# GpSimd makes the low part of a weight piece in two halves of 512 columns, and TensorE waits for each half

## The reference, cut to what matters

```python
for l in range(2):                                   # first block
    x = x + 0.5 * rmsnorm(swiglu(rmsnorm(x, g), w_gate[l], w_up[l], w_down[l]), g)   # 1024 -> 2816 -> 1024
    x = x + rmsnorm(token_mixing(rmsnorm(x, g), w_in[l], ..., w_out[l]), g)          # three kinds of attention
    x = x + 0.5 * rmsnorm(swiglu(...), g)
for l in range(2):                                   # second block
    x = x + merged(rms_norm(x), mem, ...) @ w_out[l]      # sparse, gated-linear and memory attention
    x = x + square(relu(rms_norm(x) @ w_up[l])) @ w_down[l]                          # 1024 -> 4096 -> 1024
```

## Time and profile before

| | |
|---|---|
| median of 3 runs | 1881.97 us (1881.95 to 1882.25) |
| the profiled execution | 1882.18 us, span 1880.7 us |
| TensorE busy | 1874.1 us (100%), weight loads 1549.2 us (82%) |
| GpSimd busy | 1554.2 us (83%) |
| ScalarE, VectorE busy | 1035.2 us, 1032.0 us (55% each) |
| weights read | 346.11 MB, 185 GB/s |

### The profile page before, as it was taken

One profiled execution on the slowest core, in us unless ns is written; L12 is line 12 of the kernel. 1 busy time (PEld: TensorE's weight loads), 2 busy tenths in 40 slices (PEclk: granted clock), 3 DMA queues, 4 the chain that ended last, 5 costly groups with the idle time before them and its releaser, 6 DMA issues.

```text
span 1880.7 us, 27121 instructions
## 1 busy us (share of the span) xinstructions
PE 1874.1 (100%) x9604; PEld 1549.2 (82%) x9604; DVE 1032.0 (55%) x2654; ACT 1035.2 (55%) x1765; POOL 1554.2 (83%) x1091
## 2 busy tenths in 40 slices
PE   9999999999999999999999999999999999999999
PEld 8888887888888889788888877888888877788887
DVE  5438465533676756554444677446444477645542
ACT  7445666444644476654466454665456554566543
POOL 8988876988798878698879787779887968778986
DMA  7665534666675554367556343456757443355664
GB/s 290 238 231 185 163 134 158 194 196 191 206 236 192 192 167 136 133 218 260 194 189 252 124 146 119 151 184 218 237 191 264 164 127 132 125 167 190 192 195 140
DMA packets 98419, 348.94 MB, mean 186 GB/s; under 512 B 13260, under 2 KB 13932, under 8 KB 97772
## 3 DMA queue, kind: packets, MB, share of 16 engines
q1 hardware_dynamic: 97708, 346.06, 55.2%
q10 hardware_dynamic: 576, 1.14, 0.2%
HBM read 346.11 MB, written 1.05 MB: 185 GB/s over the span
## 4 chain that ended last, share of the span: by engine, by line
PE 98%; POOL 1%; DVE 0%; ACT 0%; issue 0%; ACTq 0%
PE psum L642 28%; PE psum L644 28%; PE psum L643 28%; PE psum L670 1%; PE psum L672 1%; PE psum L673 1%; PE psum L911 1%; PE psum L728 1%; PE psum L901 1%; PE psum L924 1%; PE psum L1170 1%; POOL lo L615 1%; PE psum L891 0%; PE psum L1327 0%; PE psum L1121 0%; PE psum L798 0%
## 5 line engine op out<-in xcount | busy, mean ns | idle before, releaser
L615 POOL TENSOR_TENSOR lo<-raw,hi 128x256 fp32r<-128x256 f32 (+1 forms) x1081 | 1546.4, 1454 | 308.5 <-ACT hi L1475 280.8
L1475 ACT ACTIVATE hi<-raw 128x1024 fp32r<-128x1024 f32 (+1 forms) x613 | 639.3, 1053 | 498.2 <-PE psum L644 460.9
L642 PE MATMUL psum<-hi,h_hi 128*128 128x512 f32 (+1 forms) x1504 | 593.0, 394 | 0.5 <-POOL lo L615 0.5
L644 PE MATMUL psum<-hi,h_lo 128*128 128x512 f32 (+1 forms) x1504 | 583.6, 388 | 0.0
L643 PE MATMUL psum<-lo,h_hi 128*128 128x512 f32 (+1 forms) x1504 | 583.0, 388 | 0.0
L2177 DVE STREAM_TRANSPOSE psum<-big 32x128 f32<-32x128 f32 (+1 forms) x960 | 344.0, 358 | 14.2
L642 PEld LDWEIGHTS psum<-hi,h_hi 128*128 128x128 f32 x1504 | 282.5, 188 | 61.7 <-POOL lo L615 2.7
L644 PEld LDWEIGHTS psum<-hi,h_lo 128*128 128x128 f32 x1504 | 282.3, 188 | 58.6
L642 PE MATMUL psum<-hi,y_hi 128*128 128x512 f32 x832 | 328.1, 394 | 0.0
L643 PEld LDWEIGHTS psum<-lo,h_hi 128*128 128x128 f32 x1504 | 282.7, 188 | 55.0
L644 PE MATMUL psum<-hi,y_lo 128*128 128x512 f32 x832 | 324.3, 390 | 0.0
(11 more groups left out here) (354 smaller groups left out, 1568.7 us busy)
## 6 DMA issues: line engine op xcount, KB each, us to landing
raw<-in_stream SPq DMA_DIRECT2D x607, 512.0 KB, 4.2
big<-in_w SPq DMA_DIRECT2D x14, 512.0 KB, 7.3
big<-in_post SPq DMA_DIRECT2D x6, 512.0 KB, 5.1
special<-in_b_merge SPq DMA_DIRECT2D x2, 1536.0 KB, 8.2
raw<-in_stream SPq DMA_DIRECT2D x8, 296.0 KB, 6.4
memkv<-in_mem_turned SPq DMA_DIRECT2D x2, 1024.0 KB, 6.3
big<-in_band SPq DMA_DIRECT2D x2, 768.0 KB, 6.3
raw<-in_first SPq DMA_DIRECT2D x2, 512.0 KB, 4.3
```

Source lines behind the costliest of these rows:

```text
L615: t = pool.tensor_tensor(M.lo[:, slot, w], M.raw[:, slot, w], f32(M.hi[:, slot_hi, w]), ALU.subtract)
L642: pe.matmul(out, lhs_hi, rhs_hi, start=start, stop=False)
L644: return pe.matmul(out, lhs_lo, rhs_hi, start=False, stop=stop)
L1475: act.activation(M.hi[:, slot_hi, used], M.raw[:, slot, used], ACT.Copy).then_inc(sem["hi"], 1)
```

## The change

Pieces from 3 on that are outside the mixers' strips and of full width (449 of them) are now two instructions of 512 columns on GpSimd. The left one raises "half_lo", the right one "lo". TensorE waits for "half_lo" ahead of the left columns and for "lo" ahead of the right ones. Quartered and narrow pieces, the end of a gated feed-forward and `high_first` wait as before. In `enter`, the wait for a piece is left out for the second token tile.

```diff
+def by_halves(c):
+    return c >= FIRST_HALVES and not in_mixer(c) and half_width(c) == PIECE // 2
+
+def halves_until(c):
+    return FIRST_HALVES + sum(by_halves(i) for i in range(FIRST_HALVES, c + 1))
...
         pool.wait_ge(sem["hi"], c + 1)
+        if by_halves(c):
+            for i in range(2):
+                w = slice(512 * i, 512 * i + 512)
+                pool.tensor_tensor(M.lo[:, slot, w], M.raw[:, slot, w], f32(M.hi[:, slot_hi, w]),
+                                   ALU.subtract).then_inc(sem["lo"] if i else sem["half_lo"], 1)
+            continue
...
+    def wait_left(c):
+        if by_halves(c):
+            pe.wait_ge(sem["half_lo"], halves_until(c))
+        else:
+            pe.wait_ge(sem["lo"], c + 1)
+
+    def wait_right(c):
+        if by_halves(c):
+            pe.wait_ge(sem["lo"], c + 1)
...
     def strip_piece(c, j, a_hi, a_lo, bank, memory=None):
-        pe.wait_ge(sem["lo"], c + 1)
+        wait_left(c)
...
         for i in range(2):
+            if i:
+                wait_right(c)
...
     def rows(...):
-        pe.wait_ge(sem["lo"], c + 1)
+        wait_left(c)       # and wait_right(c) between the halves of m == 0
...
     def half_rows(c, m, kt, a_hi, a_lo, banks, stop):
         if m == 0:
-            pe.wait_ge(sem["lo"], c + 1)
-        t = rows_tile(c, m, kt, a_hi, a_lo, banks, False, stop)
+            wait_left(c)
+        t = rows_tile(c, m, kt, a_hi, a_lo, banks, False, stop, lambda: None if m else wait_right(c))
...
     def enter(...):
-                pe.wait_ge(sem["lo"], c + j + 1)
+                if m == 0:
+                    wait_left(c + j)       # and wait_right between the halves, in strip_tile and rows_tile
```

More of the change, by code:

```diff
@@ L687, in rows, with right_half @@
     def rows(c, kt, a_hi, a_lo, banks, start, stop=False, second=lambda: None, right=lambda m: None):
-        pe.wait_ge(sem["lo"], c + 1)
+        def right_half(m):
+            if m == 0:
+                wait_right(c)
+            right(m)
+        wait_left(c)
         for m in range(MT):
@@ L692, in rows @@
                 second()
-            t = rows_tile(c, m, kt, a_hi, a_lo, banks, start, stop, lambda: right(m))
+            t = rows_tile(c, m, kt, a_hi, a_lo, banks, start, stop, lambda: right_half(m))
             if stop and m == 0:
@@ L735, in enter @@
             for j in range(4):
-                pe.wait_ge(sem["lo"], c + j + 1)
+                if m == 0:
+                    wait_left(c + j)
                 pe.wait_ge(sem["xlo"], 8 * f + 4 * m + pair_of(j) + 1)
@@ L748, in strip_tile @@
         for i in range(2):
+            if i and m == 0:
+                wait_right(c)
             k, w = 2 * j + i, slice(i * 512, i * 512 + 512)
@@ L1415, in mix2 @@
                 enter(V.merged, (0, 1, 2, 3), "merged", 4 * layer, c,
-                      lambda cc, m, j: rows_tile(cc, m, j, h_hi, h_lo, (4, 6), j == 0, False), lambda j: j // 2)
+                      lambda cc, m, j: rows_tile(cc, m, j, h_hi, h_lo, (4, 6), j == 0, False,
+                                                 lambda: None if m else wait_right(cc)), lambda j: j // 2)
                 pe.wait_ge(sem["xlo"], 8 * n["feats"])
```

## The result

The changed kernel is slower. Five runs of it have a median of 1890.76 us (1889.64 to 1890.95), the kernel before took 1882.14 us beside them (1881.95 to 1882.91). The ratio on record is 1.0042, 95% interval 1.0031 to 1.0053; the two medians themselves stand 8.6 us or 0.46% apart. The forecast was 1880.1 us and "no change"; the result lies outside its range and on the side that had a chance of 0.05. The profiled execution took 1890.49 us with a span of 1889.0, 8.3 us more than the span before.

A forecast was written before the change was run, and what follows sets the result against it. TensorE was taken as the bound, busy 1874.1 of 1880.7 us. Removing six short waits (1.44 us) and shrinking two longer ones (0.46) gave 1.9 us off the median 1881.97: 1880.1 us, range 1878.9 to 1882.3.

The forecast's parts named there:

- GpSimd's added time: On GpSimd, 449 pieces become 898 instructions: 0.15 us more per piece, 67 us in all, costing nothing beside TensorE.
- The pair: Two halves of one piece on GpSimd, forecast to take 2.51 us by the spacing of starts.
- The six short waits: TensorE's waits for low parts at the fourth piece of an `enter`; all go, 6 x 0.24 = 1.44 us gained.
- The two longer ones: TensorE's waits at pieces 407 and 551, second block's mixer; move to the right half and shrink, 2 x 0.23 = 0.46 us.
- TensorE's extra waits: One more TensorE wait per whole piece, 449 in all, ahead of the right columns; forecast to cost nothing, at most 22 us.
- the eight borders: The six short and two longer TensorE waits for low parts together; forecast gain 1.44 + 0.46 = 1.9 us.
- rival 1: At the eight waits, the right half's wait takes the whole gain; time stays at 1882.0 us; chance 0.20.
- rival 3: At the eight waits, a cut costs only 0.06 us and all waiting goes: 2.5 us gained, 1879.5 us; chance 0.10.
- rival 4: TensorE's added waits hold up its start; at 0.02 us each 7 us slower, 1889 us; chance 0.02.
- rival 2: GpSimd becomes the bound in feed-forwards once a pair costs over 0.25 us extra; at 0.30, 22 us, 1904; chance 0.03.
- The section on what is late next: Near the eight borders, transpositions waiting for VectorE's x don't take the gain; GpSimd's 0.45 us delay before quartered pieces ends there.

The follow-up runs named there:

- Experiment 6: Changed kernel, all 449 pieces halved, with VectorE's whole group of small angle operations moved to strips 6 to 10 of the feed-forward before; 1880.49 us, ratio 0.9988.
- Experiment 3: Changed kernel, with GpSimd waiting for its own last result before each of pieces 164 to 229 (one feed-forward); 1885.45 us, ratio 1.0014.
- experiment 4: Changed kernel with halves on GpSimd only; TensorE waits for the whole piece as in the kernel before; 1894.62 us, ratio 1.0062.
- experiment 7: Changed kernel, with GpSimd waiting for its own last result before each of pieces 174 to 203 only; 1882.68 us, ratio 1.0005.
- experiment 2: Changed kernel, with only VectorE's cast of the positions moved to strip 7 of the first layer's feed-forward; 1890.51 us, ratio 1.0041.
- experiment 8: Kernel before, no halves added, with VectorE's small angle operations one strip earlier; 1891.88 us, ratio 1.0044.

## Why the prediction was wrong, point by point

**What held.** GpSimd's added time: 898 instructions of 1302 ns, busy 1614.3 us where 1620 stood. The pair: 40 halves in 49.90 us start (49.90 - 1.30) / 39 = 1.246 us apart, 2.49 per pair (2.51 forecast). The six short waits: -0.24 each, whole gap gone. The two longer ones: they moved to the right half, 0.40 us of load idle time, and shrank by 0.27 (0.23 forecast). TensorE's extra waits: nothing. Experiment 6, where nothing else disturbs these terms, gave their sum: 1.9 to 2.0 us at the eight borders for 1.9 forecast, and 2.05 us between the medians. Rivals 1, 3 and 4 fell with this; rival 2 too in its own form, since GpSimd never made TensorE wait in the changed kernel. Experiment 3 shows that it was close: another 0.18 us per pair brought it about, and at the price that the rival gave, 66 x (0.33 - 0.25) = 5.3 us for 5.8 measured. (The lower end of the range should read 1878.8; its own terms, 1879.5 less 0.7, give that.)

**The step that failed** is the costing of GpSimd's added time at nothing: "It lies beside TensorE as long as GpSimd has idle time", and "That cover is thin but there". The arithmetic on the earlier trace rows was right as an average, and it asked the wrong question twice. It asked only whether TensorE would be short of low parts, not who else waits for GpSimd to pause. And it spread the idle time evenly, while the trace has it in stretches: after each start of a stage GpSimd is behind and works without a break until it has caught up. How long that takes is a quotient. Before, it gains 2.72 - 2.36 = 0.36 us per piece and needs 17 pieces from 498.32 on, so by this estimate it had about 17 x 0.36 = 6.1 us to make up. With halves it gains 2.72 - 2.49 = 0.23 and needs some 6.1 / 0.23 = 27 pieces; experiment 6 shows 29. Six per cent more work per piece, and the run is 1.7 times as long. The product behind the cast was wanted 14.4 us after the cast began. Before, the run had 10.4 us left, and the product was done at 540.55, 1.8 us ahead of its matmul at 542.43: covered, and so invisible in every wait. After, the run had over 40 us left (to 570.89, by experiment 6), and the product could not be in time.

The section on what is late next failed with it. It looked at operands of TensorE near the eight borders and at GpSimd's own queue; VectorE's queue stood in no step. Yet the section ahead of the prediction says why the quartered pieces have waits among them, "so that VectorE gets in between", and in both kernels GpSimd waits for its own last piece ahead of every quartered one (`pool.wait_ge(sem["lo"], c)`). The whole pieces have no such wait, and no step asked what VectorE does beside them. The row that gave it away was on record in the trace before:

```profile
L2804 DVE CAST small<-small 128x3 f32<-128x3 int32 x1 | 10.5, 10452 | 0.0
```

Its idle time is 0.0 and it delays nobody, so it appears in no view of waits. Only its mean beside its 128x3 is out of line.

**The rest of the ledger.** The last transposition of a short border now has its matmul 0.03 us behind, as a border without a wait has. The +0.45 us at pieces 488 to 490 is one new wait of 0.3 us for a quartered piece (L631) and what follows it; +0.56 at the start of the kernel was in 0.49 already at the ninth piece. Neither follows from the halves alone: experiments 4, 6 and 7 halve the same pieces ahead of the second place and have no such shift there (-0.03 us), and experiments 2, 3 and 7, with the same halves at the start, begin 0.2 to 0.3 us earlier than the kernel before. What causes them is open.

**Which operations are held.** In the same run VectorE's transpositions into PSUM (0.33 us each) and the subtraction from PSUM to `y_lo` (0.69 us) keep their time. Those held were a cast of 3 columns, a multiply of 8, and a multiply of 1024 columns, with SBUF on both sides. This case's traces agree with half of what the Trainium skill states. SBUF — State Buffer, section "Who interferes with whom", says that VectorE and GpSimd share a pair of SBUF ports as an exclusive lock, that copies, casts and tensor_scalar operations can take the form that needs it, and that the order of issue decides who blocks. By its words the lock is held for an instruction, so a cast would wait at most the 2.4 us of a whole or 1.3 us of a half, and halving would shorten every such wait. Where GpSimd is not behind, the runs agree: the median multiply of 1024 columns (L2830 before, L2869 after) takes 2.88 us beside wholes and 1.78 beside halves. Within a backlog they differ: 10.45, 20.20, 14.16 and 11.33 us, always to the end of the run. A short pause for GpSimd's own completion lets VectorE in (1.19 us).

**A long run alone does not hold it.** In the changed kernel GpSimd has another unbroken run, as many halves long as the cast had to wait for, and a large operation of VectorE falls into it:

```profile
629.84 21.42 POOL L621 TENSOR_TENSOR lo<-raw,hi 128x512 fp32r<-128x512 f32 x16 [0.84 <-ACT hi L1514]
635.15 4.94 DVE L2869 TENSOR_SCALAR big<-big 128x1024 f32<-128x1024 f32 x3
```

Its three instructions take 1.5 to 1.8 us each, about one half of GpSimd's per turn. The difference is the backlog. Near 635 us GpSimd starts its pieces 0.3 to 0.6 us after ScalarE's high part is ready. The piece that it had in work when the cast arrived had been ready for 3.2 us in the changed kernel, 1.9 before and 3.1 in experiment 8, and it was 1.6 at the held multiply of experiment 7. In the ten traces there are eight operations held like this, and beside them none from SBUF to SBUF that took over 2.3 us more than the shortest of its form, which is less than one whole piece.

**What stays open.** Why a waiting VectorE operation gets no turn between two instructions of a backlog, although GpSimd's starts are 0.13 us further apart per cut than its columns explain, was not tried. Nor do the runs say how large the backlog must be, between the 0.6 us that let VectorE in and the 1.6 that did not, nor which kinds of operation besides the three are held by it. That the ports are what the two engines share is the page's statement; the runs show the dependence and its release, not the circuit.

## What to carry to other kernels

Look in the list of costliest lines for an instruction whose duration is out of line with its size, even if nobody waits for it: here it was a wait on another engine, with a cover that the change took away. When an engine gets slower per piece, don't ask for its share of busy time but for the length of its run after a start of a stage, backlog / (pitch of the taker - its own pitch), where pitch is the time from one piece to the next, and for what the neighbours do within it. Split work only at the pieces whose first part someone waits for: eight of 449 gave 2.55 us here, and all 449, with VectorE's operations out of the way, 2.05.

## What the runs showed of the hardware that was not expected

- An operation of VectorE from SBUF to SBUF, of 3 columns even, waited for the end of GpSimd's run where GpSimd had a backlog: 10.45 us behind the last 4 or 5 whole pieces of a run, 20.20 us behind 16 halves, 14.16 us in the kernel before with an earlier operation. The two ends agree to 0.02 us. In an unbroken run of 16 halves without such a backlog three multiplies of 1024 columns took 1.5 to 1.8 us each.
- A wait of GpSimd for its own completion opens a gap for VectorE (1.19 us instead of 20.20) and costs 0.18 us per pair of halves.
- A stop of TensorE of 7 to 8 us costs more than itself: matmuls start 0.43 us apart at a granted clock of 0.50, the 1.2 GHz level, for 3.0 us after it in the change and 4.7 to 5.1 us in experiments 2, 4 and 8. That costs 1.5 us in the change and 2.3 to 2.5 in the others.
